# Output projection's last two units one after the other, and the first FFN's first pair with its early channel tiles in a row

## The chip, the cores and the metric

## The reference

A decoder trunk of two layers over 1024 tokens of 1024 channels. Only the end of the first layer's mixer and the start of its FFN matter here:

```python
x = x + even_mixer(rms_norm(x, e_norm_g[j]), ...)      # ends in: y_cat @ w_out
x = x + conv_ffn(rms_norm(x, f_norm_g[i]), f_w_up[i], f_conv_w[i], f_conv_b[i], f_w_down[i])

def rms_norm(x, g):
    x32 = x.astype(jnp.float32)
    y = x32 * lax.rsqrt(jnp.mean(x32 * x32, axis=-1, keepdims=True) + NORM_EPS)
    return (y * g.astype(jnp.float32)).astype(x.dtype)

def conv_ffn(xn, w_up, conv_w, conv_b, w_down):
    h = causal_dwconv(xn @ w_up, conv_w, conv_b)
    gate, val = jnp.split(h, 2, axis=-1)
    return (jax.nn.silu(gate) * val) @ w_down
```

`w_out` is 1024 x 1024, `w_up` is 1024 x 5632 (gate and value halves of 2816).

## The kernel before

Data lie channel-major: a *tile* is 128 channels by 1024 tokens, and `x_res` holds the eight tiles of the residual stream. Every large product is made in three parts, for precision: an operand is split into a rounded high part and the rest, and hi x hi, hi x rest and lo x hi are summed. So each weight block is cast by ScalarE (high part) and then subtracted by GpSimd (low part), and each activation block is cast by ScalarE and subtracted by VectorE (its *rest*, `rest_dve`).

**Output projection.** A *unit* is one tile of the output: 8 input tiles x 3 parts x 2 token halves = 48 matmuls. Its weights come in two chunks of 4 input tiles, which SyncE loads into two places in turn (`load_out`), ScalarE casts (`take_hi`) and GpSimd subtracts (`take_lo`). Units 0 to 5 go one by one (`unit_products`, in a loop from the third on). Units 6 and 7 go side by side (`halves_products`): input tiles 0 to 3 of unit 6, then of unit 7, then tiles 4 to 7 of unit 6, then of unit 7. VectorE adds each finished unit to `x_res` (`residual_add_dve`). For the norm ScalarE squares each tile (`square_act`) and VectorE adds the squares up (`sum_dve`).

**The FFN's up product** is made in *pairs*: one gate tile and one value tile, each split into token halves, by seven block products in place of eight. The eight channel tiles are four pairs j = 0 to 3 (tiles 2j and 2j + 1); from each pair's four blocks b11, b12, b21, b22 VectorE makes four differences t1 to t4 (`sum_blocks`), after ScalarE has scaled the blocks by the norm's gain (`scale_act`). The seven products take the operands b11, t1, t2, t4, b21, t3, b22 in this order (`ORDER`; the text calls the first four the first to fourth product). Each has four parts, one for each j, of three matmuls of 512 columns: 12 matmuls a product. The weights of the seven products lie in a ring of four places; two of these places are the projection's own weight places, and one is in the memory of the projection's operand. GpSimd makes weight sums and low parts, in the order of `before_last_pool` and `pair_pool`.

**Memory.** The blocks of j = 2 and the b11 block of j = 3 (`x7_late`) lie where the projection's input tiles 0 to 3 lie; the rest of j = 3 lies where input tiles 4 to 7 lie. They may be written when TensorE has read these for the last time. So ScalarE waits, before it scales j = 2, until both units' first chunks are done.

**The first pair** (`first_pair_pe`) is written out by hand, since its operands come late: TensorE takes parts j = 0 and 1, then 2, then 3 as they are ready. After the fifth product come the column sums of squares (16 small matmuls, `sums_pe`), three transposes for tables of the next layer (this FFN only: `self.tables`), the sixth product (t3), the broadcast of the root over the partitions (`wide_pe`: four matmuls), and the seventh product (b22). Between sums and broadcast ScalarE takes the root and VectorE the reciprocal and a spread copy (`rows_dve`). Then 21 more pairs follow.

The work between the projection's end and the first pair is ordered by hand in `before_out_act`, `out_blocks_act`, `first_pair_act` on ScalarE, in `before_out_dve`, `between_out_dve`, `last_blocks_dve`, `first_pair_dve` on VectorE. The second FFN has the same pairs behind another layer's products, and other such functions; of the edited ones it shares only the `else` branch of `first_pair_pe` and `first_pair_dve`. Two lines show the waits that count:

```python
dn.wait_unit(act, final - 1, 1)        # before_out_act: unit 7's first chunk done (side by side)
self.scale_act(act, 3, "b11", *x_done) # j = 3, b11: after unit 6's residual add
```

Of the kernel before, what the change touches and what calls it, by code (L numbers as in the profile page):

```python
# [21 lines left out]
DT = D_MODEL // P  # L22
# [39 lines left out]
def trunk(nc, io, out):  # L62
# [923 lines left out]
    with ExitStack() as sc:  # L986
# [5 lines left out]
        dn = Dense(sc, "e")  # L992
# [569 lines left out]
    with ExitStack() as sc:  # L1562
# [45 lines left out]
        def load_out(sp, raw, n, chunk, unit):  # L1608
            sp.wait_ge(w_lo_done, 2 * EV + n + 1)
            sp.dma_start(raw[:, n % 2, :, :], w_out[:, KC * (1 - chunk):KC * (2 - chunk), unit * P:unit * P + P]).then_inc(  # L1610
                w_loaded[n % 2], 16)
# [75 lines left out]
    c_hi, c_lo = (at(f"c_{n}", [P, DT, SEQ], C_AT + 8 * k * TILE, F32R) for k, n in enumerate(("hi", "lo")))  # L1687
# [217 lines left out]
    ORDER = (0, 2, 1, 6, 3, 4, 5)  # L1905
    POS = {k: p for p, k in enumerate(ORDER)}
    BLOCK = ("b11", "t2", "t1", "b21", "t3", "b22", "t4")
# [11 lines left out]
    class Ffn:  # L1919
# [258 lines left out]

        def first_pair_pe(self, pe):
            self.after_rest(pe, 1, "high")  # L2180
            self.part_pe(pe, 0, 0, 0, 2)
            self.after_rest(pe, 2, "low")
            self.part_pe(pe, 0, 0, 2, 3)
            self.after_rest(pe, 3, "b11")
            self.part_pe(pe, 0, 0, 3, 4)
            self.part_pe(pe, 0, 2, 0, 3)
            self.after_rest(pe, 3, "t1")
            self.part_pe(pe, 0, 2, 3, 4)
            self.part_pe(pe, 0, 1, 0, 3)
            self.part_pe(pe, 0, 6, 0, 3)  # L2190
            self.after_rest(pe, 3, "t2")
            self.part_pe(pe, 0, 1, 3, 4)
            self.after_rest(pe, 3, "t4")
            self.part_pe(pe, 0, 6, 3, 4)
            self.after_rest(pe, 3, "b21")
            self.part_pe(pe, 0, 3)
            self.nm.sums_pe(pe)
            if self.tables:
                self.tables.turn_pe(pe)
            self.after_rest(pe, 3, "t3")  # L2200
            self.part_pe(pe, 0, 4)
            self.nm.wide_pe(pe)
            self.after_rest(pe, 3, "b22")
            self.part_pe(pe, 0, 5)
# [291 lines left out]
        def before_out_act(self, act, final, x_done):  # L2496

            dn = self.dn
            dn.take_hi(act, DT, final, 0, 0, 1)
            self.w_hi_act(act, 0)  # L2500
            dn.take_hi(act, DT, final, 0, 1, 2)
            dn.wait_unit(act, final - 1, 1)
            for b in ("b11", "b12", "b22", "b21"):
                self.scale_act(act, 2, b)
            self.scale_act(act, 3, "b11", *x_done)
            self.cast_act(act, 2, "low")
            self.scale_act(act, 3, "b12")
            self.w_hi_act(act, 1)
            self.cast_act(act, 2, "high")
            self.cast_act(act, 3, "b11")  # L2510
            self.nm.square_act(act, DT - 2)

        def out_blocks_act(self, act, final, x_done):

            self.dn.wait_unit(act, final, 1)
            self.cast_act(act, 3, "t1")
            self.w_hi_act(act, 2)
            act.wait_ge(*x_done)
            self.scale_act(act, 3, "b22")
            self.scale_act(act, 3, "b21")  # L2520
            self.w_hi_act(act, 3)
            self.cast_act(act, 3, "t2")
            self.snap_act(act, 0, "p1")
            self.w_hi_act(act, 4)
            self.cast_act(act, 3, "t4")
            self.cast_act(act, 3, "b21")
            self.nm.square_act(act, DT - 1)

        def before_out_dve(self, dve):
            for t in ("t1", "t2", "t4", "t3"):  # L2530
                self.sum_blocks(dve, 2, t)

        def between_out_dve(self, dve):
            self.rest_dve(dve, 2, "low")
            self.sum_blocks(dve, 3, "t1")
            self.rest_dve(dve, 3, "b11")
            self.rest_dve(dve, 2, "b21")
# [111 lines left out]

        def first_pair_dve(self, dve):  # L2650
            self.evac_dve(dve, 0, "u2")
            if self.tables:
                self.nm.sum_dve(dve, DT - 2)
            self.nm.sum_dve(dve, DT - 1)
            self.rest_dve(dve, 2, "top")
            self.rest_dve(dve, 3, "t3")
            self.rest_dve(dve, 3, "b22")
            self.nm.rows_dve(dve)
            if self.tables:
                self.tables.angles_dve(dve, 2)  # L2660
            dve.wait_ge(ln_kept, self.nm.late + 1)
            for name in ("c22", "c21", "val"):
                self.evac_dve(dve, 0, name)
# [33 lines left out]
    def residual_add_dve(dve, dn, c, slot, pair, par):  # L2697

        dn.wait_unit(dve, pair, par)
        here = x_res[:, bass.ds(c, 1), :]  # L2700
        nc.vector.tensor_tensor(here, here, dn.acc[slot][:, :], ALU.add).then_inc(unit_free, 1)
# [497 lines left out]
    with ExitStack() as sc:  # L3199
# [182 lines left out]
        with nc.Block() as block:  # L3382
            @block.sync
            def _(sp):
# [2 lines left out]
                for k, name in enumerate(("o_A_re", "o_A_im")):  # L3387
                    sp.dma_start(s_rows[:, k, :], io[name].rearrange("a (r g) n -> (a r) (g n)", g=2)).then_inc(s_loaded, 16)
                sp.dma_start(dt_rows[:, :], io["o_log_dt"].rearrange("a (r g) -> (a r) g", g=2)).then_inc(s_loaded, 16)
                for unit in range(2, DT - 2):  # L3390
                    for chunk in range(2):
                        load_out(sp, dn.raw, 2 * unit + chunk, chunk, unit)
                for chunk in range(2):
                    for s in range(2):
                        load_out(sp, dn.raw, 2 * (DT - 2 + chunk) + s, chunk, DT - 2 + s)
                    if chunk == 0:
                        ffn0.begin_sp(sp)
                ffn0.load_sp(sp)

# [62 lines left out]
            def _(pool):  # L3462
# [4 lines left out]
                with pool.Fori(1, DT // 2 - 1) as i:  # L3467
                    for s in range(2):
                        dn.take_lo(pool, DT, i * 2 + (u_out + s), 0)
                dn.take_lo(pool, DT, out_end, 0)  # L3470
                ffn0.before_last_pool(pool)
                dn.take_lo(pool, DT, out_end + 1, 0)
                ffn0.lo_pool(pool)
                for n in range(DT):
                    for chunk in range(2):
# [19 lines left out]
            def _(pe):  # L3495
# [7 lines left out]
                out_products(pe, 1, 0, KC)  # L3503
                out_products(pe, 2, KC, DT)
                out_products(pe, 3, KC, DT)
                with pe.Fori(1, DT // 2 - 1) as i:
                    for s in range(2):
                        for chunk in range(2):
                            unit_products(dn, pe, DT, c_hi, c_lo, i * 2 + (u_out + s), s, chunk, y_ready)
                halves_products(pe, out_end, c_hi, c_lo, y_ready)  # L3510
                ffn0.products_pe(pe)

                def states_pe(i):
# [184 lines left out]
            def _(dve):  # L3698
# [11 lines left out]
                for c in range(DT - 2):  # L3710
                    residual_add_dve(dve, dn, c, c % 2, *((u_out + c, 1) if c else (u_out + 1, 0)))
                    ffn0.block_dve(dve, c)
                ffn0.before_out_dve(dve)
                residual_add_dve(dve, dn, DT - 2, 0, out_end + 1, 0)
                ffn0.between_out_dve(dve)
                residual_add_dve(dve, dn, DT - 1, 1, out_end + 1, 1)
                ffn0.last_blocks_dve(dve)
                ffn0.work_dve(dve)
                tables.link.close()
# [106 lines left out]
```

## Time and profile before

| | us |
|---|---|
| median of 3 runs | 2570.85 (2568.71 to 2570.9) |
| profiled execution, whole | 2569.76 |
| its span on the core | 2566.3 |
| mean granted TensorE clock | 0.991 |
| last two output units on TensorE | 728.56 to 750.32 |
| first pair of the first FFN on TensorE | 750.32 to 784.25 |

Times in the rows are microseconds from the start of the span. A row of a timeline gives start, duration (from the first to the last of the instructions merged in it), engine, source line, operation, output and inputs, and how many; in brackets how long the engine had been idle before it, and which engine and line ended the wait. Matmuls are pipelined: one of 512 columns lasts 0.39 us in the record but the next begins 0.227 us later.

### The profile page before, as it was taken

Reading aid. Unit: us, or ns where it says so; the run is one execution under the profiler, and the core shown is the slowest. Engines: PE = TensorE matmul, PEld = TensorE weight load, DVE = VectorE, ACT = ScalarE, POOL = GpSimd, SP = SyncE. Lnnn points to the kernel's source line nnn. Section 1 sums busy time; section 2 is a strip of 40 time slices with the busy share of each in tenths; the row PEclk is TensorE's granted clock in tenths of the full one; section 3 lists DMA queues with packets and bytes.
Section 4 is the critical chain, followed back from the end, with each engine's and each line's share of the span. In section 5 each row is a group of like instructions: output and inputs, shape, how many; then the busy total and the mean of one; then the engine's idle time right before and its main releaser. Section 6 shows DMA issues by size and latency. Waiting matters only on the chain. (4 is left out here: it accounts for less than half of the span.)

```text
span 2566.3 us, 33658 instructions
## 1 busy us (share of the span) xinstructions
PE 2461.1 (96%) x12861; PEld 2049.7 (80%) x12861; DVE 1463.5 (57%) x1902; ACT 1108.4 (43%) x1782; POOL 1307.2 (51%) x1072
## 2 busy tenths in 40 slices
PE   8999899999999998999999999989999999999997
PEld 6788788888777786888778878978878888888886
DVE  6441578877556667566566546654375565562223
ACT  5442344544444543455144444433265454452222
POOL 5323445454246775875268644412367777762221
PEclk9999999999999999999999999999999999999998
DMA  3112000000111222223445424531212222243312
GB/s 107 46 39 60 21 1 2 1 1 1 42 58 58 91 74 66 83 85 126 116 167 201 139 90 144 174 106 54 61 49 88 78 82 90 75 140 107 111 50 86
DMA packets 249504, 203.46 MB, mean 79 GB/s; under 512 B 25061, under 2 KB 228359, under 8 KB 247303
## 3 DMA queue, kind: packets, MB, share of 16 engines
q1 hardware_dynamic: 235143, 179.63, 22.4%
q10 hardware_dynamic: 14208, 21.76, 2.4%
q8 instruction: 99, 1.62, 0.3%
q14 instruction: 54, 0.44, 0.1%
HBM read 148.92 MB, written 48.23 MB: 77 GB/s over the span
## 5 line engine op out<-in xcount | busy, mean ns | idle before, releaser
L198 POOL TENSOR_TENSOR dense_lo<-dense_raw,dense_hi 128x512 fp32r<-128x512 f32 (+2 forms) x142 | 175.4, 1236 | 465.9 <-ACT dense_hi L191 465.6
L191 ACT CAST dense_hi<-dense_raw 128x512 fp32r<-128x512 f32 (+2 forms) x142 | 79.3, 565 | 393.1 <-PE acc_o L1716 144.2
L2111 POOL TENSOR_TENSOR dense_lo<-w_raw_l,dense_hi 128x512 fp32r<-128x512 f32 x88 | 118.2, 1343 | 63.9 <-ACT dense_hi L2107 63.7
L2111 POOL TENSOR_TENSOR dense_lo<-w_sums_l,dense_hi 128x512 fp32r<-128x512 f32 x66 | 103.1, 1563 | 72.9 <-ACT dense_hi L2107 72.9
L2111 POOL TENSOR_TENSOR w_l<-w_raw_l,w_l 128x512 fp32r<-128x512 f32 x88 | 114.9, 1305 | 46.7 <-ACT w_l L2107 46.7
L198 POOL TENSOR_TENSOR w_lo_e<-w_raw_e,w_hi_e 128x512 fp32r<-128x512 f32 x42 | 56.4, 1345 | 158.1 <-ACT w_hi_e L191 158.1
L404 PE MATMUL main_ps<-rounded 128*128 128x256 f32 x896 | 128.1, 294 | 8.9 <-DVE rounded L299 8.9
L404 PEld LDWEIGHTS main_ps<-rounded 128*128 128x128 f32 x896 | 113.6, 190 | 27.3 <-DVE rounded L299 23.3
L2111 POOL TENSOR_TENSOR w_l<-w_sums_l,w_l 128x512 fp32r<-128x512 f32 x66 | 104.0, 1575 | 45.1 <-ACT w_l L2107 45.1
L2257 PE MATMUL bank_b<-h_hi_l,dense_hi 128*128 128x512 f32 x352 | 109.9, 394 | 6.2 <-POOL dense_lo L198 5.8
L2173 PE MATMUL acc_o<-x_early_l,dense_hi 128*128 128x512 f32 x352 | 108.7, 390 | 3.4 <-POOL dense_lo L2111 3.4
L2173 PE MATMUL bank_a<-x_early_l,w_l 128*128 128x512 f32 x396 | 104.5, 400 | 7.4 <-POOL w_l L2111 7.4
L2257 PE MATMUL bank_b<-h_lo_l,dense_hi 128*128 128x512 f32 x352 | 109.3, 392 | 0.0
L2257 PE MATMUL bank_b<-h_hi_l,dense_lo 128*128 128x512 f32 x352 | 108.8, 391 | 0.0
L2173 PE MATMUL acc_o<-x_late_l,dense_hi 128*128 128x512 f32 x352 | 108.3, 389 | 0.0
L2633 DVE TENSOR_TENSOR bank_b<-bank_b,p_kept_later_l 128x512 f32<-128x512 f32 x44 | 28.5, 695 | 139.8 <-ACT p_kept_later_l L2367 139.8
L2257 PE MATMUL bank_a<-h_hi_l,dense_hi 128*128 128x512 f32 x336 | 105.2, 394 | 2.0 <-DVE h_lo_l L2391 1.3
L2689 DVE TENSOR_TENSOR x_res<-x_res,bank_a 128x1024 f32<-128x1024 f32 x28 | 34.2, 1220 | 126.8 <-PE bank_a L2257 126.8
L2173 PE MATMUL bank_a<-x_late_l,w_l 128*128 128x512 f32 x396 | 104.0, 399 | 1.2 <-DVE x_late_l L2071 1.2
L2257 PE MATMUL bank_a<-h_lo_l,dense_hi 128*128 128x512 f32 x336 | 103.7, 390 | 0.0
L2257 PE MATMUL bank_a<-h_hi_l,dense_lo 128*128 128x512 f32 x336 | 103.5, 389 | 0.0
L2173 PE MATMUL acc_o<-x_early_l,w_l 128*128 128x512 f32 x396 | 100.9, 390 | 2.0 <-ACT p_kept_l L2367 1.9
(545 smaller groups left out, 7035.4 us busy)
## 6 DMA issues: line engine op xcount, KB each, us to landing
w_raw_l<-in_f_w_up SPq DMA_DIRECT2D x176, 256.0 KB, 3.0
hidden<-val SPq DMA_DIRECT2D x44, 512.0 KB, 2.6
h_f_l<-hidden SPq DMA_DIRECT2D x44, 512.0 KB, 4.7
w_raw_e<-in_e_w_in SPq DMA_DIRECT2D x42, 256.0 KB, 2.9
dense_raw<-in_f_w_down SPq DMA_DIRECT2D x40, 256.0 KB, 2.9
dense_raw<-in_f_w_down SPq DMA_DIRECT2D x48, 192.0 KB, 2.6
s_states<-t_hx ACTq DMA_DIRECT2D x16, 512.0 KB, 2.9
s_inputs<-t_in ACTq DMA_DIRECT2D x16, 512.0 KB, 3.0
```

The costliest lines, as they stand in the source:

```text
L191: nc.scalar.copy(self.hi[:, par, 0:n, :], self.raw[:, par, 0:n, :]).then_inc(w_hi_done, 1)
L198: pool.tensor_tensor(self.lo[:, par, 0:n, :], self.raw[:, par, 0:n, :], self.hi[:, par, 0:n, :].bitcast(F32), op=ALU.subtract).then_inc(w_ ...
L404: return nc.tensor.matmul(bank[:, at:at + 2 * CH], lhs, rhs, skip_group_check=True, **flags)
L2111: pool.tensor_tensor(self.ring_lo[n % 4], self.source(ORDER[n % SEVEN]), self.ring_hi[n % 4].bitcast(F32), op=ALU.subtract).then_inc(q_lo, 1)
L2173: last = nc.tensor.matmul(bank, w[n % 4][:, j, :], x(j, BLOCK[k]), start=begins and j == 0 and w is self.ring_hi and x == self.x_hi, stop= ...
L2257: last = nc.tensor.matmul(self.down_acc[s][:, h * HALF:(h + 1) * HALF], place[w][:, t, :], x[here][:, h * HALF:(h + 1) * HALF], start=begi ...
L2633: nc.vector.tensor_tensor(here, here, kept, ALU.mult if kept.shape[-1] == SEQ else ALU.add).then_inc(q_evac, 1)
L2689: nc.vector.tensor_tensor(here, here, self.down_acc[c % 2][:, :], ALU.add).then_inc(unit_free, 1)
```

## The change

1. Units 6 and 7 of the projection go one by one, as a third turn of the loop. SyncE loads their chunks in that order, GpSimd makes the low part of unit 7's first chunk ahead of the FFN's first weight sums, and unit 6's residual add waits for its own second chunk.
2. ScalarE squares tile 6 before it scales the blocks of j = 2, and these scales now wait for unit 7's first chunk. The second product's high weights come right behind these scales, those of the third and fourth come before the t1 cast. VectorE adds the square of tile 6 first (it stood behind the first evacuation), and the low rest of j = 2 comes ahead of the residual add of tile 7.
3. In the first FFN's first pair TensorE takes j = 0 and 1 of the first four products, then j = 2 of all four, then j = 3 of all four.

```diff
         def first_pair_pe(self, pe):
             self.after_rest(pe, 1, "high")
+            if self.tables:
+                for k in ORDER[:4]:
+                    self.part_pe(pe, 0, k, 0, 2)
+                self.after_rest(pe, 2, "low")
+                for k in ORDER[:4]:
+                    self.part_pe(pe, 0, k, 2, 3)
+                for k in ORDER[:4]:
+                    self.after_rest(pe, 3, BLOCK[k])
+                    self.part_pe(pe, 0, k, 3, 4)
+            else:
...
...
         (before_out_act)
-            dn.wait_unit(act, final - 1, 1)
+            act.wait_ge(*x_done)
+            self.nm.square_act(act, DT - 2)
+            dn.wait_unit(act, final, 0)
             for b in ("b11", "b12", "b22", "b21"):
                 self.scale_act(act, 2, b)
-            self.scale_act(act, 3, "b11", *x_done)
+            self.w_hi_act(act, 1)
+            self.scale_act(act, 3, "b11")
             self.cast_act(act, 2, "low")
             self.scale_act(act, 3, "b12")
-            self.w_hi_act(act, 1)
             self.cast_act(act, 2, "high")
             self.cast_act(act, 3, "b11")
-            self.nm.square_act(act, DT - 2)
...
         (out_blocks_act)
             self.dn.wait_unit(act, final, 1)
+            self.w_hi_act(act, 2)
+            self.w_hi_act(act, 3)
             self.cast_act(act, 3, "t1")
-            self.w_hi_act(act, 2)
             act.wait_ge(*x_done)
             self.scale_act(act, 3, "b22")
             self.scale_act(act, 3, "b21")
-            self.w_hi_act(act, 3)
             self.cast_act(act, 3, "t2")
+            self.cast_act(act, 3, "t4")
+            self.cast_act(act, 3, "b21")
             self.snap_act(act, 0, "p1")
             self.w_hi_act(act, 4)
-            self.cast_act(act, 3, "t4")
-            self.cast_act(act, 3, "b21")
             self.nm.square_act(act, DT - 1)
...
         def before_out_dve(self, dve):
+            self.nm.sum_dve(dve, DT - 2)
             for t in ("t1", "t2", "t4", "t3"):
                 self.sum_blocks(dve, 2, t)
+            self.rest_dve(dve, 2, "low")
 
         def between_out_dve(self, dve):
-            self.rest_dve(dve, 2, "low")
...
         (first_pair_dve)
             self.evac_dve(dve, 0, "u2")
-            if self.tables:
-                self.nm.sum_dve(dve, DT - 2)
             self.nm.sum_dve(dve, DT - 1)
...
         (SyncE)
-                for unit in range(2, DT - 2):
+                for unit in range(2, DT):
                     for chunk in range(2):
                         load_out(sp, dn.raw, 2 * unit + chunk, chunk, unit)
-                for chunk in range(2):
-                    for s in range(2):
-                        load_out(sp, dn.raw, 2 * (DT - 2 + chunk) + s, chunk, DT - 2 + s)
-                    if chunk == 0:
+                    if unit == DT - 2:
                         ffn0.begin_sp(sp)
...
         (GpSimd)
                 dn.take_lo(pool, DT, out_end, 0)
+                dn.take_lo(pool, DT, out_end + 1, 0, 0, 1)
                 ffn0.before_last_pool(pool)
-                dn.take_lo(pool, DT, out_end + 1, 0)
+                dn.take_lo(pool, DT, out_end + 1, 0, 1, 2)
...
         (TensorE)
-                with pe.Fori(1, DT // 2 - 1) as i:
+                with pe.Fori(1, DT // 2) as i:
                     for s in range(2):
                         for chunk in range(2):
                             unit_products(dn, pe, DT, c_hi, c_lo, i * 2 + (u_out + s), s, chunk, y_ready)
-                halves_products(pe, out_end, c_hi, c_lo, y_ready)
...
         (VectorE)
+                residual_add_dve(dve, dn, DT - 2, 0, out_end, 1)
                 ffn0.before_out_dve(dve)
-                residual_add_dve(dve, dn, DT - 2, 0, out_end + 1, 0)
+                residual_add_dve(dve, dn, DT - 1, 1, out_end + 1, 1)
                 ffn0.between_out_dve(dve)
-                residual_add_dve(dve, dn, DT - 1, 1, out_end + 1, 1)
```

## Rows read from the trace of the kernel before

**Rows 1.** The page: span, TensorE's busy time.

```profile
span 2566.3 us, 33658 instructions
PE 2461.1 (96%) x12861; PEld 2049.7 (80%) x12861; DVE 1463.5 (57%) x1902; ACT 1108.4 (43%) x1782; POOL 1307.2 (51%) x1072
```

**Rows 2.** Timeline of TensorE, around the first pair.

```profile
655.37 1.10 PE L3304 MATMUL bank_a<-p_even,centre 128*128 128x512 f32 x2 [0.94 <-PEq L1620]
...
728.56 0.61 PE L2711 MATMUL acc_o<-c_hi,dense_hi 128*128 128x512 f32 x2
...
750.32 1.52 PE L2173 MATMUL bank_a<-x_early_l,w_l 128*128 128x512 f32 x6
...
753.74 0.98 PE L2173 MATMUL bank_a<-x_late_l,w_l 128*128 128x512 f32 x3 [1.22 <-DVE x_late_l L2071]
...
768.51 1.91 PE L1767 MATMUL acc_o<-ssum,pick 128*8 128x128 f32 x16 [2.60 <-DVE ssum L1759]
...
772.39 0.73 PE L2173 MATMUL bank_b<-x_early_l,dense_hi 128*128 128x512 f32 x2 [1.66 <-DVE x_late_l L2071]
...
776.31 2.73 PE L1789 MATMUL acc_o<-sq,ones_row 8*128 8x512 f32 x4 [0.91 <-DVE sq L1782]
...
784.25 0.63 PE L2173 MATMUL acc_o<-x_early_l,dense_hi 128*128 128x512 f32 x2
```

**Rows 3.** Timeline of TensorE, end of the second FFN's first pair.

```profile
1892.19 0.73 PE L2173 MATMUL bank_b<-x_early_l,dense_hi 128*128 128x512 f32 x2 [1.40 <-DVE x_late_l L2071]
...
1896.11 1.98 PE L1789 MATMUL acc_o<-sq,ones_row 8*128 8x512 f32 x4 [0.90 <-DVE sq L1782]
```

**Rows 4.** Busy time of TensorE by window, then its granted clock.

```profile
766.00:777.00 11.00, 5.91 (x33) 1.00 0.02 7
777.50:784.00 6.50, 6.50 (x14) 0.50 0.00 0
1019.80:1023.00 3.20, 0.39 (x2) 1.00 0.00 0
1023.50:1026.50 3.00, 3.00 (x8) 0.50 0.59 173
...
1716.00:1719.40 3.40, 3.40 (x10) 0.51 0.00 0
1728.90:1735.00 6.10, 3.87 (x17) 1.00 0.30 86
```

**Rows 5.** Windows of both first pairs: PE, PEld, DVE, ACT, POOL, clock.

```profile
750.32:784.25 33.93, 27.54 (x108) 19.51 (x107) 28.47 (x26) 16.97 (x27) 21.70 (x13) 0.90 0.08 24
...
1873.40:1900.80 27.40, 23.70 (x106) 17.55 (x105) 23.11 (x18) 14.87 (x24) 20.06 (x12) 1.00 0.10 30
```

**Rows 6.** Timeline of VectorE, from the last units on.

```profile
743.79 0.69 DVE L2046 TENSOR_TENSOR x_late_f_l<-x_late_f_l,spread 128x512 f32<-128x512 f32 x1
745.08 1.22 DVE L2701 TENSOR_TENSOR x_res<-x_res,acc_o 128x1024 f32<-128x1024 f32 x1 [0.61 <-PE acc_o L2711]
748.89 2.29 DVE L2064 TENSOR_TENSOR x_late_l<-x_late_f_l,x_late_l 128x2048 fp32r<-128x2048 f32 x1 [2.59 <-ACT x_late_l L2052]
...
757.85 4.98 DVE L2071 TENSOR_TENSOR x_late_l<-x_late_f_l,x_late_l 128x512 fp32r<-128x512 f32 x3
...
773.96 0.93 DVE L1778 RECIPROCAL rstd_rows<-rstd_rows 8x128 f32<-8x128 f32 x1
774.92 1.33 DVE L1782 TENSOR_TENSOR sq<-rstd_rows,ident 8x1024 f32<-8x1024 f32 x1
```

**Rows 7.** Timeline of GpSimd.

```profile
736.72 1.30 POOL L2123 TENSOR_TENSOR w_raw_l<-w_raw_l 128x512 f32<-128x512 f32 x1
...
750.07 2.27 POOL L2111 TENSOR_TENSOR dense_lo<-w_sums_l,dense_hi 128x512 fp32r<-128x512 f32 x1 [8.38 <-ACT dense_hi L2107]
...
781.25 1.28 POOL L2111 TENSOR_TENSOR dense_lo<-w_sums_l,dense_hi 128x512 fp32r<-128x512 f32 x1 [6.07 <-ACT dense_hi L2107]
```

**Rows 8.** Timeline of ScalarE.

```profile
739.70 0.62 ACT L191 CAST dense_hi<-dense_raw 128x512 fp32r<-128x512 f32 x1 [4.30 <-PE acc_o L2711]
...
766.60 0.62 ACT L2107 CAST dense_hi<-w_raw_l 128x512 fp32r<-128x512 f32 x1
...
771.12 1.28 ACT L1773 ACT_TABLE_LOAD   x1
```

## Prediction before the run

> **What bounds the kernel now.** The page comes first: TensorE is busy for 2461.1 of the 2566.3 us span [rows 1], so a change outside its gaps is worth nothing. The stage is then found in TensorE's timeline [rows 2]. The last two output units are 96 matmuls from 728.56 to 750.32 without a gap, 0.2267 us each. The first pair of the first FFN follows, from 750.32 to 784.25. Its work at full clock is 84 matmuls of products (19.04 us), 1.9 for the column sums, 0.35 for the three transposes, and 1.9 for the row broadcast (1.98 in the second FFN [rows 3]): 23.2 us of the 33.9. The other 10.7 are:
>
> - a gap of 1.4 before 753.74, for the fourth tile's b11 rest (the ninth matmul began at 752.13, so 752.36 was due);
> - 2.8 before 768.51, for VectorE's last sum of squares;
> - 1.7 before 772.39, for the t3 rest; 1.2 before 776.31, for the spread row;
> - 3.3 of slow clock: broadcast and b22 product take 784.25 - 776.31 = 7.9 where 4.6 are due. The granted clock is 0.50 from 777.5 to 784, the 1.2 GHz level, after a stretch with 5.91 of 11.0 us busy [rows 4].
>
> The same pair in the second FFN takes 27.4 us, all at clock 1.00 [rows 5]. That is the size of what order can bring here. In the timelines of the other engines the reader is to see that VectorE has no idle time from 748.89 to 776: 28.5 of 33.9 us busy [rows 5, 6]. It runs slower than alone: a 512-column operation on two SBUF tensors takes 0.69 (743.79) but three take 4.98 beside GpSimd (757.85), and GpSimd's 1.30 becomes 2.27 beside VectorE's 2.29 [rows 6, 7]. One waits out the other. I cost such a pair as the sum less 0.2 to 0.3.
>
> **Units one by one.** TensorE's 96 matmuls keep their number and pace, and the places are filled and freed at the same times (734.00, 739.44, 744.88, 750.32); SyncE loads the same sizes in the same queue positions, so this part costs nothing there. A loop's third turn replaces straight code, and what TensorE meets behind the loop is new. It leaves the loop without a gap now (728.56); between two blocks of the program its sequencer cost 0.94 at 655.37 [rows 2]. I take 0 and keep 0.9 for the range. GpSimd takes the low part of unit 7's first half at 734.9 before its first sums, which end at 738.6, then 1.3 each for the first low part and the third sum: 741.2, then the last half's low part at 742.5, due at 744.88. That is hidden, with 2.4 to spare. The raw load behind the third sum moves 3 us later (the sum ended at 738.0 [rows 7]); its data are first used at 766.60 [rows 8].
>
> Two times move. Unit 6 is whole at 739.44, not 744.88, so its residual add (1.22 [rows 6]) ends at 740.9, its square at 741.9, and VectorE's seventh sum of squares at 743.5. This takes an operation of 1.2 alone, 1.7 beside GpSimd, out of the crowded stretch. But both units now read the early four channel tiles until 744.88, and the third tile's blocks lie in that memory: their four scales move from 740.22 to 745.15.
>
> **The stretch behind it, step by step.** ScalarE reacts 0.26 after a matmul group (739.70 after 739.44 [rows 8]).
>
> - ScalarE: four scales at 0.63 each 745.15 to 747.65, second product's high weights 748.2, fourth tile's b11 748.8.
> - VectorE: t1, t2, t4 from 746.5 to 748.5; GpSimd's second low part takes 748.3 to 749.6 and pushes t3 to 750.1 (749.4 if they don't meet).
> - ScalarE: low cast 1.8 (750.15 to 752.0), scale b12 0.6, high cast 1.4, b11 cast 0.5: 754.5. Then the third product's high weights, 755.0, and the fourth's, 755.5.
> - GpSimd: the third low part, 755.1 to 756.4; the fourth, beside VectorE, until 758.0.
> - TensorE: products one and two take their early tiles from 750.32 to 753.04, and the third waits for its low weights until 756.4: **a new gap of 3.4**. The early part costs another 0.3 before the fourth. The third tiles need the low rest, there at 754.3, and cause no wait. The gap before b11 (1.4) is gone.
> - VectorE: low rest 752.0 to 754.3, last residual 755.4, three operations beside GpSimd until 760.3, seven alone at 0.66 until 764.9 (each rest's cast is ready: t1's at 757.5, t2's at 762.2), evacuation 765.5.
> - TensorE: 24 more matmuls from 759.5 end at 764.9, the four last ones just behind their rests. Then b21 waits for its low weights: ScalarE has casts until 763.4, the copy 763.9, the high weights 764.4, and GpSimd needs until 766.0. Gap 1.2; b21 runs 766.1 to 768.8.
> - VectorE's last sum of squares ends at 767.1, so the column sums abut b21: 768.8 to 770.7. The gap of 2.8 is gone. Transposes 771.1, t3 rest 770.9: the gap of 1.7 is gone, and t3 ends at 773.8.
> - The root: copy 0.6, table load 1.28, root 0.36 after 770.7 [rows 8]: 773.2; reciprocal 0.93 and spread 1.33 [rows 6], with one meeting with GpSimd: 776.3. Gap 2.5 (was 1.2).
>
> Reckoned in this way the order before gives 776.0 where 776.31 was measured, so I take 776.5 for the broadcast: 0.2 later than now. New gaps sum to 7.5 against 7.1. **In queue time the change is nothing; the clock decides.**
>
> **The clock.** A gap of 2.8 at 1019.8 to 1023 (0.39 of 3.20 us busy) was followed by clock 0.50; one of 2.2 within 1728.9 to 1735 was not, and the 2.8 before 768.51 was not at once [rows 2, 4]. The new gap of 3.4 is on the wrong side. A slow stretch there lasts some 3.4 us, as the one from 1716 (clock 0.51): the third and fourth products' early parts lose 1.7, of which 0.8 is absorbed by the later waits for rests, so the broadcast begins at 777.4. Towards the end, the column sums no longer follow a gap, and from 764.9 to the broadcast TensorE has two full products (5.4 us) where it had one (2.7). The second FFN has that shape: sums, a gap of 1.4, t3, a gap of 0.9, broadcast in 1.98 at full clock [rows 3]. So I take it that the late slow stretch goes, and end at 777.4 + 4.6 = 782.0 instead of 784.25: **2.2 faster**.
>
> The Trainium skill (TensorE: Matmul & The Clock Gate, HAM oscillation — how this bites in real kernels) says that a wait between bursts of matmuls can put the engine back to its slow clock; it speaks against gathering gaps into one, and the trace agrees at 1019.8. It is priced in the first rival from rows alone.
>
> Behind 784 nothing gives the shift back: the third low weights of the next pair are made from 781.25 [rows 7] and due 5.4 us after its start, and they follow the broadcast, so they move with it.
>
> **Rivals.**
> - *Both slow stretches* (the early gap lowers the clock and the late stretch stays, as the 2.5 gap before the broadcast could do): 777.4 + 7.9 = 785.3, **+1.1**; with an early stretch of 6.8, as the late one now is, +2.8. For it: three idle stretches ahead of the broadcast remain. Against: the second FFN's tail. It passes the measurement's limit of 5.1 us only if the third product's low weights come 2.3 us later still.
> - *No slow stretch*: t3's sum doesn't meet GpSimd, the first gap is 2.7, under the smallest that lowered the clock. 776.5 + 4.6 = 781.1, **-3.1**, with 0.7 more from the earlier casts -3.8. Against: GpSimd's start at 748.3 falls inside the sums.
> - *Only the late one*: 784.4, **+0.2**. The change then does nothing, since VectorE and ScalarE together set the pair's end and a re-ordering of TensorE moves only where it waits.
> - *The seventh sum's removal is worth its full 1.7*: VectorE was the queue without idle time, and the late scales cost nothing if its waits are elsewhere. Then the root starts earlier and it is -4 to -5. Against: the low cast is 3.1 later and VectorE stands idle until 752.0.
>
> **Numbers.** Chances: early stretch only 0.40, both 0.27, late only 0.12, none 0.15, the last rival 0.06. The profiled execution took 2569.76 us, 3.5 more than its span, and the likeliest case puts it at 2567.6. The median of the runs, 2570.85, lies 1.1 above it (runs from 2568.71), and the prediction is made on the median: 2570.85 - 2.2 = 2568.7. Range: the cases give -4.5 to +2.8, or 2566.3 to 2573.7; with 0.8 more below for the spread of medians, 2565.5 to 2573.7. The likeliest case's own range is 2567 to 2570. A difference within 0.2% (5.1 us) can't be told from no change; the gain side passes it only with the last rival or a lower median (0.12), the loss side with both stretches and a longer wait (0.07).
>
> **What the profile should show.** The third tile's four scales at 745.1; the square of tile 6 before them; a gap in TensorE's row near 753 of 2.7 to 3.8 us that ends with GpSimd's low part; no idle time between the b21 product and the column sums; a gap of 2 to 3 before the broadcast; VectorE idle before the low rest. The prediction is wrong if the low cast starts before 749, if the first gap is over 5 us, or if the pair lasts under 29 or over 38 us.

## The result, and the profile after

The changed kernel took 2573.86 us (median of 22 runs, 2572.04 to 2579.11); the kernel before took 2569.8 in the 22 runs beside it (2564.37 to 2577.2). The ratio is 1.0018, with a 95% interval of 1.001 to 1.0025: on 2569.8 that is 4.6 us slower (2.6 to 6.4); the two medians lie 4.1 apart. The forecast was 2.2 us faster, likeliest 2568.7, range 2565.5 to 2573.7; the median is 0.16 above the range. The ratio is inside the 0.2% to which the prediction gave 0.81, but its interval leaves out no change, so that 22 runs tell a difference that the prediction held to be too small to tell, and its sign is the other one. The profiled execution took 2575.68 us.

The page of the changed kernel: span and TensorE's busy time, 5.7 us more than in [rows 1] with the same number of matmuls.

```profile
span 2573.6 us, 33667 instructions
PE 2466.8 (96%) x12861; PEld 2054.7 (80%) x12861; DVE 1461.0 (57%) x1902; ACT 1108.5 (43%) x1782; POOL 1306.1 (51%) x1072
```

Timeline of TensorE in the first pair. The pair starts at 751.37 here and at 750.32 in [rows 2]; that 1.05 lies ahead of the change, so 1.05 is to be taken off before a time is laid beside the prediction's.

```profile
751.37 1.52 PE L2173 MATMUL bank_a<-x_early_l,w_l 128*128 128x512 f32 x6
...
753.87 0.39 PE L2173 MATMUL bank_a<-x_early_l,dense_lo 128*128 128x512 f32 x1
757.84 2.38 PE L2173 MATMUL bank_b<-x_early_l,w_l 128*128 128x512 f32 x6 [3.59 <-POOL w_l L2111]
...
768.49 1.62 PE L2173 MATMUL bank_a<-x_early_l,w_l 128*128 128x512 f32 x6 [0.57 <-issue]
...
771.42 1.91 PE L1767 MATMUL acc_o<-ssum,pick 128*8 128x128 f32 x16
773.26 0.37 PE L2805 MATMUL acc_o<-ident,s_rows 32*128 32x32 f32 x3
773.56 0.73 PE L2173 MATMUL bank_b<-x_early_l,dense_hi 128*128 128x512 f32 x2
...
778.75 3.56 PE L1789 MATMUL acc_o<-sq,ones_row 8*128 8x512 f32 x4 [2.17 <-DVE sq L1782]
782.24 2.93 PE L2173 MATMUL bank_a<-x_early_l,w_l 128*128 128x512 f32 x6
784.97 1.96 PE L2173 MATMUL bank_a<-x_late_l,w_l 128*128 128x512 f32 x6
786.76 0.63 PE L2173 MATMUL acc_o<-x_early_l,dense_hi 128*128 128x512 f32 x2
```

The reader sees the predicted schedule: one gap of 3.59 for the third product's low weights, nothing between b21 and the column sums (771.42) nor before the t3 rest (773.56), one gap of 2.17 before the broadcast. What is not as predicted is the broadcast's own duration, 3.56 us where 1.98 was put in.

Windows of TensorE: start and end, length, busy time (instructions), granted clock, DMA share, GB/s. They are the pair; the stretch ahead of the broadcast; from the broadcast to the next pair; and the third and fourth products' early parts.

```profile
751.37:786.76 35.39, 29.06 (x108) 0.86 0.08 23
766.00:777.00 11.00, 10.00 (x52) 1.00 0.17 48
778.75:786.70 7.95, 7.95 (x16) 0.57 0.01 2
757.84:762.20 4.36, 4.36 (x12) 0.61 0.20 60
```

There are two slow stretches, both at the 1.2 GHz level for most of their length. Busy time by (1 - clock) is what each lost: 4.36 x 0.39 = 1.7 us behind the first gap, 7.95 x 0.43 = 3.4 us from the broadcast on.

The chain that leads to the 3.59, in ScalarE's timeline (first fence), VectorE's (second) and GpSimd's (third):

```profile
746.13 0.73 ACT L2028 ACTIVATE x_late_f_l<-x_res,prm 128x512 f32<-128x512 f32 x1 [3.12 <-PE acc_o L1716]
...
751.52 1.91 ACT L2052 CAST x_late_l<-x_late_f_l 128x2048 fp32r<-128x2048 f32 x1 [1.69 <-DVE x_late_f_l L2046]
...
755.84 0.61 ACT L2107 CAST w_l<-w_sums_l 128x512 fp32r<-128x512 f32 x1
```

```profile
749.71 1.78 DVE L2046 TENSOR_TENSOR x_late_f_l<-x_late_f_l,spread 128x512 f32<-128x512 f32 x1
```

```profile
749.28 1.65 POOL L2111 TENSOR_TENSOR dense_lo<-w_sums_l,dense_hi 128x512 fp32r<-128x512 f32 x1 [5.56 <-ACT dense_hi L2107]
756.53 1.26 POOL L2111 TENSOR_TENSOR w_l<-w_sums_l,w_l 128x512 fp32r<-128x512 f32 x1 [5.59 <-ACT w_l L2107]
```

The scales start behind the early tiles' last use, VectorE's t3 block meets GpSimd (1.78 us, where 0.69 is the price alone [rows 6]), ScalarE waits 1.69 us for it with its low cast, and the third product's high weights stand at the end of ScalarE's row, at 755.84. GpSimd has been idle for 5.59 us when they come.

### The profile page after: what moved, and what is told of

It reads as the page before. It is cut to its first block and busy times, and to the rows that moved or that the text cites. A ratio compares the mean times of both kernels' runs of the same rounds, so it can differ in the third digit from the quotient of the medians.

```text
span 2573.6 us, 33667 instructions
## 1 busy us (share of the span) xinstructions
PE 2466.8 (96%) x12861; PEld 2054.7 (80%) x12861; DVE 1461.0 (57%) x1902; ACT 1108.5 (43%) x1782; POOL 1306.1 (51%) x1072
## 5 line engine op out<-in xcount | busy, mean ns | idle before, releaser
L404 PEld LDWEIGHTS main_ps<-rounded 128*128 128x128 f32 x896 | 113.5, 190 | 27.4 <-DVE rounded L299 23.3
```

Of the source, the lines that this page charges most:

```text
L404: return nc.tensor.matmul(bank[:, at:at + 2 * CH], lhs, rhs, skip_group_check=True, **flags)
```

## The experiments

The quoted expectations name the theories by letters. Theory A is the accounting of queue times and clock stretches from the profiles; the other letters are its rivals of that run. Each ratio is against the kernel before on the same chip; it is estimated over the runs and need not be the quotient of the two medians. "Idle matmuls" are 128x512 products of data already there, written to a bank that the next real product starts afresh; no experiment leaves out any of the work. Lines are of TensorE's timeline unless another view is named.

**TensorE's new order alone.** The kernel before, with only the part order changed:

```
             self.after_rest(pe, 1, "high")
+            if self.tables:
+                for k in ORDER[:4]:
+                    self.part_pe(pe, 0, k, 0, 2)
+                self.after_rest(pe, 2, "low")
+                for k in ORDER[:4]:
+                    self.part_pe(pe, 0, k, 2, 3)
+                for k in ORDER[:4]:
+                    self.after_rest(pe, 3, BLOCK[k])
+                    self.part_pe(pe, 0, k, 3, 4)
```

> Only TensorE's new order in the first pair, on the queues of before. Theory A (the order of TensorE's parts and the clock carry the loss, the queues' time is unchanged by the change as a whole): the third product's low weights come at 755.8 here, so a gap of 2.7 opens before it and the b11 part runs last of the early ones; ScalarE's copy of the first product (p1) waits 9 us longer ahead of the t4 and b21 casts, so the pair's broadcast starts 4 us later than in before: 4 to 6 us slower than before. Rival B (units one by one carry the loss, the order is free): same as before within 1 us.

2578.11 us against 2571.84, ratio 1.0026 (1.0016 to 1.0036), 6.7 us on 2571.84.

```profile
758.69 1.65 PE L2173 MATMUL bank_b<-x_early_l,w_l 128*128 128x512 f32 x6 [1.75 <-POOL w_l L2111]
761.76 0.73 PE L2173 MATMUL bank_b<-x_early_l,dense_hi 128*128 128x512 f32 x2 [1.42 <-POOL dense_lo L2111]
...
775.56 1.91 PE L1767 MATMUL acc_o<-ssum,pick 128*8 128x128 f32 x16 [1.93 <-DVE ssum L1759]
```

The order asks for the third and fourth products' low weights before the low rest, and the old queues of ScalarE and GpSimd make them late. And without the new queues it takes little away: the wait for VectorE's sum of squares still stands, now 1.93 where it was 2.60 [rows 2]. The broadcast starts 30.13 us into the pair, 4.1 later than in [rows 2], as Theory A had it; the time is a little above its 4 to 6 us, and Rival B (no difference) is out.

**The units one by one, and the new queues of the others, alone.** The changed kernel with TensorE's old order:

```
-            if self.tables:
+            if False:
                 for k in ORDER[:4]:
```

> The change without TensorE's new order in the first pair (units one by one, and the new queues of ScalarE, VectorE and GpSimd). Theory A: the first product now waits for the low rest (2.6 us later than before) and for b11, early gaps of about 2.6 and 4; the broadcast starts 1.4 later than in the changed kernel: 5 to 7 us slower than before. Rival B: as slow as the changed kernel, 3 to 5 us slower than before, since the order doesn't matter.

2573.73 us against 2571.84, ratio 1.0015 (1.0005 to 1.0025), 3.9 us on 2571.84; the two medians lie only 1.9 apart.

```profile
758.64 0.99 PE L2173 MATMUL bank_a<-x_late_l,w_l 128*128 128x512 f32 x3 [2.91 <-DVE x_late_l L2064]
762.90 1.65 PE L2173 MATMUL bank_a<-x_late_l,w_l 128*128 128x512 f32 x3 [3.27 <-DVE x_late_l L2071]
...
782.79 1.98 PE L1789 MATMUL acc_o<-sq,ones_row 8*128 8x512 f32 x4 [0.96 <-DVE sq L1782]
...
787.55 0.62 PE L2173 MATMUL acc_o<-x_early_l,dense_hi 128*128 128x512 f32 x2
```

The late scales show as two waits, 2.91 for the low rest and 3.27 for the fourth tile's b11. The broadcast is 28.58 us into the pair, later than in the changed kernel (27.38), and yet this profile's pair is shorter, 33.34 against 35.39: the gap ahead of the broadcast is 0.96 and the broadcast takes 1.98. A slow stretch is here too: the granted clock is 0.50 from 759.5, just behind the 2.91 wait, through the 3.27 one and to 766.0. Theory A's 5 to 7 us did not come, and the time alone does not speak against Rival B.

Each half of the change costs time by itself, and together (1.0018) they cost less than the sum of the two. What the new order adds to the new queues isn't shown, since 1.0015 and 1.0018 differ by less than their intervals.

**The changed kernel's gaps filled.** Twelve idle matmuls after the second product's early tiles, eight before the broadcast:

```
+        def fill_pe(self, pe, n):
+            bank = self.banks[1][0][:, 0:HALF]
+            for _ in range(n):
+                nc.tensor.matmul(bank, self.x_hi(0, "b11")[:, 0:P], self.x_hi(0, "b11"), start=True, stop=True,
+                                 skip_group_check=True)
...
                     self.part_pe(pe, 0, k, 0, 2)
+                    if k == 2:
+                        pe.wait_ge(unit_free, self.u0 + 1)
+                        self.fill_pe(pe, 12)
...
+            if self.tables:
+                self.fill_pe(pe, 8)
             self.nm.wide_pe(pe)
```

> The changed kernel with 20 idle matmuls of 512 columns on constant data into a free PSUM bank: 12 in the gap before the third product, 8 in the gap before the root's broadcast; they leave out nothing and add nothing to the output. Theory A (the loss is slow clock): the clock stays at 1.00 through the pair; the pair gets 4 to 5 us shorter than in the changed kernel, so 0 to 2 us faster than the kernel before. Rival C (the loss is queue time, the clock only follows): the gaps are the same and the time stays 3 to 5 us above before.

2570.28 us against 2571.84, ratio 0.9997 (0.9987 to 1.0008). The loss is gone. First the timeline, then one window with its granted clock.

```profile
757.51 1.65 PE L2173 MATMUL bank_b<-x_early_l,w_l 128*128 128x512 f32 x6 [0.89 <-POOL w_l L2111]
...
777.53 1.98 PE L1789 MATMUL acc_o<-sq,ones_row 8*128 8x512 f32 x4 [0.40 <-DVE sq L1782]
```

```profile
780.50:783.80 3.30, 3.30 (x10) 0.55 0.00 0
```

The third product still waits for GpSimd and starts 6.49 us into the pair (6.47 in the changed kernel), so no work came sooner; what changed is the clock. The third product's early six took 1.65 instead of 2.38, and the broadcast came 26.51 us into the pair instead of 27.38. That 0.87 is the price of the early slow stretch in this profile, put at 0.9. The broadcast ran at full clock, and the clock fell for the b22 product instead: filling moved and shortened the late stretch (3.30 x 0.45 = 1.5 us lost in this window, not 3.4). So the full clock that Theory A expected through the pair did not come, and the pair, 32.86 us, is 2.5 shorter than the changed kernel's and not 4 to 5; Rival C (the time stays 3 to 5 above) is out.

**The gaps of the kernel before filled.** The same helper in the kernel before, ten before the sums, five before t3 and four before the broadcast:

```
+                pe.wait_ge(unit_free, self.u0 + 1)
+                self.fill_pe(pe, 10)
             self.nm.sums_pe(pe)
...
+                self.fill_pe(pe, 5)
             self.after_rest(pe, 3, "t3")
...
+                self.fill_pe(pe, 4)
             self.nm.wide_pe(pe)
```

> The kernel before with 19 idle matmuls: 10 before the column sums, 5 before the sixth product, 4 before the broadcast. Theory A: the late slow stretch of the profiled run (3.3 us) goes, and the kernel is 2 to 3 us faster than before, if that stretch is there in most executions; if it is there in half of them, 1 to 2 us. Rival C: same as before within 0.5.

2570.91 us against 2571.84, ratio 1.0 (0.9991 to 1.001). The window of the whole pair:

```profile
750.77:781.60 30.83, 28.91 (x128) 1.00 0.10 26
```

The pair is 3.1 us shorter than in [rows 5] and the clock is full throughout, but the medians are only 0.9 us apart, not 2 to 3, and the ratio shows no difference. Either something else pays it back, or the profile shown of the kernel before, from which the 33.93 comes, was not a typical one. The next two ask that.

**The kernel before, profiled twice more**, unchanged.

> The kernel before once more, for its profile: does the slow stretch at the end of the first pair come back? Theory D (the first profile of before overstated it: filling the gaps shortened the profiled pair by 3.1 us but not the timed executions, so in most executions before has no such stretch): the pair takes 30 to 31 us in this profile, clock 1.00. Theory A (it is in most executions): 33 to 34 us, as in the first profile.

> A second repeat of the kernel before, for its profile. Theory D: pair of 30 to 31 us at clock 1.00. Theory A: 33 to 34 us.

2566.35 and 2571.83 us. One fence each:

```profile
777.34 2.14 PE L1789 MATMUL acc_o<-sq,ones_row 8*128 8x512 f32 x4 [0.90 <-DVE sq L1782]
...
783.68 0.62 PE L2173 MATMUL acc_o<-x_early_l,dense_hi 128*128 128x512 f32 x2
```

```profile
769.28 2.63 PE L1767 MATMUL acc_o<-ssum,pick 128*8 128x128 f32 x16 [2.62 <-DVE ssum L1759]
...
777.95 1.98 PE L1789 MATMUL acc_o<-sq,ones_row 8*128 8x512 f32 x4
...
782.73 0.62 PE L2173 MATMUL acc_o<-x_early_l,dense_hi 128*128 128x512 f32 x2
```

The pairs last 32.32 and 31.65 us. The gaps are the same to 0.02 us where the clock is not low, yet the slow stretch is another one each time: in the first profile from 777.4, within the broadcast, to the pair's end [rows 4]; in the second from 779.0, late in the broadcast, to 782.5, half as long; in the third from 770.2, 0.9 us behind the end of the 2.62 gap, to 777.1, over before the broadcast. Neither answer that was expected fits; the truth is a spread, with a mean of 32.6 over the three. The first profile had its longest. Against that mean the filled pair (30.83) is 1.8 us shorter, which the interval of its ratio (2.3 us faster to 2.6 slower) does not exclude.

**The changed kernel, profiled twice more**, unchanged.

> The changed kernel once more, for its profile. Theory F (both slow stretches belong to it: 35.4 us in its first profile, against 31.7 to 33.9 in three of before): the pair takes 34 to 36 us, with clock 0.50 behind the first gap. Rival G (the first profile was an unlucky one, and the stretches come and go as in before): 31 to 33 us.

> A third profile of the changed kernel. Theory F: 34 to 36 us. Rival G: 31 to 33 us.

2569.21 and 2572.11 us. One fence each:

```profile
757.37 2.34 PE L2173 MATMUL bank_b<-x_early_l,w_l 128*128 128x512 f32 x6 [3.59 <-POOL w_l L2111]
...
778.27 3.52 PE L1789 MATMUL acc_o<-sq,ones_row 8*128 8x512 f32 x4 [2.17 <-DVE sq L1782]
...
786.27 0.62 PE L2173 MATMUL acc_o<-x_early_l,dense_hi 128*128 128x512 f32 x2
```

```profile
778.05 3.78 PE L1789 MATMUL acc_o<-sq,ones_row 8*128 8x512 f32 x4 [2.17 <-DVE sq L1782]
...
785.98 0.62 PE L2173 MATMUL acc_o<-x_early_l,dense_hi 128*128 128x512 f32 x2
```

The pairs last 35.38 and 35.29 us. Here there is hardly a spread: both slow stretches come in all three profiles, and each begins at the same place in the pair within 0.6 us. Theory F holds for the profiles; the two execution times lie among those of the kernel before on that chip (2568.29 to 2578.62).

**Only the last gap filled.** The changed kernel with eight idle matmuls before the broadcast (the last piece of the diff above):

> The changed kernel with 8 idle matmuls ahead of the broadcast alone (constant data, a free PSUM bank, nothing left out); the first gap stays. Theory F: the first gap's slow stretch stays (broadcast 27.1 to 27.5 after the pair's start) and the late one goes (4.6 to 5.5 us from broadcast to the next pair): 2 to 4 us faster than the changed kernel, 0 to 2 slower than before. Rival H (the early stretch carries the loss alone): less than 1 us faster than the changed kernel.

2573.37 us against 2573.22, ratio 1.0003 (0.9994 to 1.0012). Against the changed kernel's 1.0018 that is 3.9 us less, as Theory F had it and not Rival H; but the intervals (to 1.0012, and from 1.001) just overlap. The pair takes 33.23 us, 2.1 less. First the timeline, then a window:

```profile
760.46 2.93 PE L2173 MATMUL bank_b<-x_early_l,w_l 128*128 128x512 f32 x6 [3.59 <-POOL w_l L2111]
...
782.45 1.98 PE L1789 MATMUL acc_o<-sq,ones_row 8*128 8x512 f32 x4 [0.38 <-DVE sq L1782]
...
787.22 0.62 PE L2173 MATMUL acc_o<-x_early_l,dense_hi 128*128 128x512 f32 x2
```

```profile
758.50:766.00 7.50, 5.54 (x13) 0.56 0.12 35
```

The late stretch is gone, 4.77 us from the broadcast to the next pair instead of 8.0, and nothing but the 2.17 gap was touched. The early one stayed, as it should, but was twice as long in this profile as in the changed kernel's three (the clock fell at 759.3, 1.1 us before the gap's end, and in the other three 0.3 to 0.7 us behind it), and put the broadcast at 28.46 us instead of the 27.1 to 27.5 expected. Why it was longer is open.

**The weights first.** The changed kernel, with ScalarE making the third and fourth products' high weights in the time in which it waited for VectorE:

```
             self.scale_act(act, 3, "b11")
+            dn.wait_unit(act, final, 1)
+            self.w_hi_act(act, 2)
+            self.w_hi_act(act, 3)
             self.cast_act(act, 2, "low")
...
-            self.dn.wait_unit(act, final, 1)
-            self.w_hi_act(act, 2)
-            self.w_hi_act(act, 3)
             self.cast_act(act, 3, "t1")
```

> The changed kernel, but ScalarE makes the third and fourth products' high weights ahead of the low cast, while it waits for VectorE's differences anyway. Theory A: the first gap (3.6 us) goes, and with it its slow stretch; the low rest comes 1.1 us later and is just in time; the broadcast starts 1 to 2 us earlier than in the changed kernel, the pair takes 31 to 34 us in the profile; 0 to 2 us slower than before in time. Rival E (VectorE's and GpSimd's turns set the end, whatever TensorE does early): the broadcast starts at the same distance from the pair's start as in the changed kernel (27.4) and the time stays 3 to 5 us above before.

2572.05 us against 2571.78, ratio 1.0 (0.9991 to 1.0009).

```profile
776.15 2.50 PE L1789 MATMUL acc_o<-sq,ones_row 8*128 8x512 f32 x4 [2.19 <-DVE sq L1782]
...
783.86 0.83 PE L2173 MATMUL acc_o<-x_early_l,dense_hi 128*128 128x512 f32 x2
```

The 3.59 gap is gone, and the broadcast starts 24.83 us into the pair: 2.55 earlier than in the changed kernel and 1.15 earlier than before. The late slow stretch stands behind a gap of 2.19 here too, and takes the advantage over the kernel before away again: 7.7 us from the broadcast to the next pair, and a pair of 32.54 where the kernel before has 32.6 in the mean. Rival E (the broadcast stays at 27.4) is out.

**The weights first, with idle matmuls.** Six before the broadcast; and, in a second kernel, four before the low rest, five before b21 and eight before the broadcast.

> The same with 6 idle matmuls ahead of the root's broadcast (constant data, a free PSUM bank, nothing left out). Theory A: no slow stretch late either; 1 to 2 us faster than the version without them and 0 to 2 us faster than before. Rival E: as the version without them, within 0.5.

> The third and fourth products' weights ahead of the low cast, and idle matmuls in all three gaps that are left (4 before the low rest, 5 before b21, 8 before the broadcast). Theory F: clock 1.00 through the pair, pair of 29.5 to 30.5 us, 2 to 3 us faster than before. Rival E: same as before.

The first took 2570.89 us against 2571.78, ratio 0.9992 (0.9983 to 1.0001); the second 2569.74 against 2573.22, ratio 0.9986 (0.9977 to 0.9995), 3.6 us less than the kernel before (1.3 to 5.9). Of the second, the timeline and then a window:

```profile
775.88 1.98 PE L1789 MATMUL acc_o<-sq,ones_row 8*128 8x512 f32 x4 [0.42 <-DVE sq L1782]
...
782.24 0.62 PE L2173 MATMUL acc_o<-x_early_l,dense_hi 128*128 128x512 f32 x2
```

```profile
778.50:782.00 3.50, 3.50 (x11) 0.52 0.00 0
```

The pairs last 31.00 and 31.23 us; 29.5 to 30.5 at full clock was expected of the second. The clock still falls once in both, in the b22 product (in the first the granted clock is 0.50 from 781.5 to 784.5). The second is the only version whose interval lies below the kernel before; that it beats the first isn't shown, since their intervals overlap.

## Why the prediction was wrong

**What held.** The queue arithmetic, as far as its steps show in TensorE's row: each within 0.7 us. First gap 3.4 expected, 3.59 measured. Sums behind b21 without a gap, t3 without a gap: so. Gap before b21 1.2, here 0.57; before the broadcast 2.5, here 2.17. Early slow stretch behind the first gap, 1.7 lost of which 0.9 reaches the broadcast: 1.7 and 0.87. The broadcast was due 777.4 - 750.32 = 27.1 us into the pair and came at 27.4. The Trainium skill (TensorE: Matmul & The Clock Gate, HAM oscillation — how this bites in real kernels) has the engine go back to its slow clock when it waits between bursts; behind the 3.59 the trace agrees, in all three profiles. The third product's early six took 2.38, 2.34 and 2.76 us there, and 1.65 at full clock.

Two sums of the prediction are off by a little, and nothing rests on it: the losses that it lists come to 10.4 of its 10.7 us, and its new gaps to 7.4, not 7.5.

**The step that failed** is "So I take it that the late slow stretch goes", with the end at 777.4 + 4.6 = 782.0. From the broadcast to the next pair the changed kernel takes 8.0, 8.0 and 7.9 us in its three profiles. The step read the second FFN's tail as a likeness, but there the gap before the broadcast is 0.90 [rows 3], and the prediction's own schedule had 2.5 there. The busy stretch of 10.00 in 11.00 us ahead did not protect the clock. Behind the unfilled gap the stretch cost 3.4 us in each of the changed kernel's three profiles; with that gap filled it cost nothing in one kernel (late fill only) and 1.6 to 1.7 us, later, in three (the changed kernel filled, both of the weights first). So the gap sets most of the late loss, and not all of it. Where the gap is 0.96 (the units alone) the broadcast ran in 1.98. The rival "both slow stretches" had it: +1.1 for the pair against the first profile, where it was 35.39 - 33.93 = +1.5. The prediction's own test, a pair of under 29 or over 38 us, was too wide to catch this.

The step also leaned on a sorting of gaps by size that one profile cannot give. Its 2.8 at 1019.8 and 2.2 behind 1728.9 were cut short by their windows: in the timeline they are 3.08 and 2.33. And across the six profiles of the two kernels (clock in windows of 0.5 us) the same gaps outside the pair are followed by the half clock in some executions and not in others: the 2.33 in three of six, one of 2.57 near 304 in three of six, the 3.08 in five of six. So the 2.17 came with a slow stretch three times out of three; that it always does isn't shown, nor why it does so more often than those.

**The second fault is what the sum was taken against.** The 33.93 of the kernel before was one execution, with the longest pair of three. Against the mean of 32.6 the rival's end (785.3, a pair of 35.0) would have been +2.4. The median under the sum was one of 3 runs, too: 2570.85, where the 22 beside the changed kernel gave 2569.8. Laid against that, the measured 4.6 is above the worst case of the prediction (+2.8). The three profiles of each, cut at the pair (means, in us):

| | start to pair | the pair | behind it | span |
|---|---|---|---|---|
| before | 750.9 | 32.6 (33.93, 32.32, 31.65) | 1783.2 | 2566.8 |
| changed | 751.0 | 35.4 (35.39, 35.38, 35.29) | 1783.9 | 2570.2 |
| difference | +0.1 | +2.7 | +0.7 | +3.4 |

The pair accounts for 2.7 of 4.6 us measured over the runs, which is the low end of their interval (2.6 to 6.4). What lies behind the pair varies from 1780.6 to 1787.1 among these six, whichever kernel it is. Most of that is slow clock elsewhere: TensorE's busy time by (1 - clock), summed there over windows of 0.5 us, is 11.6, 9.0 and 12.2 us before and 15.6, 9.2 and 11.4 changed. Without it 1770.5, 1771.6 and 1774.8 are left before, 1771.3, 1771.6 and 1772.7 changed: no loss of the change shows there. Whether the runs hold a further part of 1 or 2 us stays open. The first profiles alone would have it otherwise: 7.3 us between the two spans, of which 4.8 lie behind the pair and are that variation.

**Where the 2.7 comes from.** In the mean the broadcast of the kernel before starts 26.3 us into the pair and that of the changed kernel 27.4: +1.1, of which the early slow stretch is 0.9. From the broadcast on, 6.3 against 8.0: +1.6, since a late stretch that before came whole in one profile, half as long in another, and in the third not behind the broadcast's start, now comes whole every time. The rest is queue time, put at +0.2: with the gaps filled the broadcast comes at 26.5 in the changed kernel, against 26.0 in the first two profiles of the one before, so +0.5 (and 0.3 of the older mean is the third profile's slow stretch, which lay ahead of the broadcast: 0.5 + 0.9 - 0.3 = 1.1). The change traded four smaller gaps for one of 3.59, one of 0.57 and one of 2.17 (6.3 us together, as TensorE's idle time in the kernel before within 0.1), and the clock set the price: slow clock cost 5.1, 5.1 and 5.0 us in the changed kernel's pairs and 3.3, 1.7 and 3.0 before.

**The other rivals.** "No slow stretch" and "only the late one" fell with the 3.59 gap and its slow clock. "The seventh sum is worth its full 1.7" fell too: the low cast came at 751.52, no earlier than the prediction had it (750.15 + 1.05 = 751.2), and VectorE stood idle 1.98 us before the low rest:

```profile
753.47 2.29 DVE L2064 TENSOR_TENSOR x_late_l<-x_late_f_l,x_late_l 128x2048 fp32r<-128x2048 f32 x1 [1.98 <-ACT x_late_l L2052]
```

A part of the gain it meant was there to be had in queue time, though: with the weights made in ScalarE's wait, the broadcast came 1.15 us earlier than before. The change lacked that place in a queue: TensorE's new order wanted the third product's weights first, and ScalarE still made them last. By itself this brings the kernel back to the time of before (1.0, 0.9991 to 1.0009) and no further, since the slow stretch behind the 2.19 gap stays.

## What to carry to other kernels

Where a forecast holds a term for a clock that falls, read that stretch in several executions first: here the same kernel lost 3.3, 1.7 or 3.0 us to it in this pair, which is as much as the whole change. When an order is changed so that small gaps gather into large ones, price each large gap by the slow stretch that it may start, at its own place, and not by a like stage whose gap is shorter. When one engine's order of products is changed, change with it the order in which the others make their operands; the place is there where an engine waits anyway.

## What the hardware showed beside it

- The broadcast (four matmuls of 8 rows) takes 1.98 us at full clock and 3.52 to 3.78 where the clock was at half for most of it. So matmuls of few rows pay as the full ones do.
- With the gaps unchanged, the kernel before had a slow stretch of another start or length in each of three profiles, while the changed kernel, with gaps of 3.59 and 2.17, had both of its in the same places three times. Other gaps of 2.33 to 3.08 us in the same six profiles were followed by the half clock in three to five of six.
- A gap of 3.59 was followed by a slow stretch of some 3.4 us in three profiles of the changed kernel and by one twice as long (0.50 from 759.5 to 766.0) in the kernel with only the late fill, which is the same up to there.
- Idle matmuls held the clock up to the broadcast, but in three of the five kernels with fills it fell 2.5 to 3 us behind the broadcast's start, amid unbroken matmuls (0.55, 0.52 and 0.50 of full speed in the windows above). In the changed kernel filled, TensorE had been busy for 12.16 of the 13.50 us ahead (766.0 to 779.5). What brings this fall, no run here shows.
